# Splitting the fp32 ones-products of a hybrid encoder step into high and low halves

## What is computed

```python
def conv_module_tail(glu, hist, conv_w, conv_b, ln_g, ln_b):
    ...
    return jax.nn.silu(layer_norm(y, ln_g, ln_b))      # mean and variance over 512 channels

def finish_layer(h, att, cv, p, w_out, g_ffn, w_gate_up, w_down, g_ple, w_ple_gate, w_ple_proj):
    h = h + jnp.concatenate([att, cv], axis=-1) @ w_out
    u = rms_norm(h, g_ffn)                             # mean square over 1024 channels
    gate, up = jnp.split(u @ w_gate_up, 2, axis=-1)
    h = h + (jax.nn.silu(gate) * up) @ w_down
    g = jax.nn.sigmoid(rms_norm(h, g_ple) @ w_ple_gate)
    return h + g * (p @ w_ple_proj)
```

## Time and profile before

| | us |
|---|---|
| median of 3 runs | 2595.95 (2593.81 to 2599.28) |
| the profiled execution | 2596.51 |
| its span, first to last instruction | 2594.8 |
| TensorE busy | 2576.0 |
| VectorE busy | 1847.3 |
| ScalarE busy | 1266.1 |

### The profile page before, as it was taken

One profiled execution on the slowest core, in us unless ns is written; L12 is line 12 of the kernel. 1 busy time (PEld: TensorE's weight loads), 2 busy tenths in 40 slices (PEclk: granted clock), 3 DMA queues, 4 the chain that ended last, 5 costly groups with the idle time before them and its releaser, 6 DMA issues.

```text
span 2594.8 us, 39909 instructions
## 1 busy us (share of the span) xinstructions
PE 2576.0 (99%) x13920; PEld 2501.2 (96%) x13920; DVE 1847.3 (71%) x3391; ACT 1266.1 (49%) x2282; POOL 590.1 (23%) x660
## 2 busy tenths in 40 slices
PE   9999999999999999999999999999999999999999
PEld 8999998999899999999999999999999999999999
DVE  3555579988878888777766877789438765766557
ACT  5444368888864323443334443423446443443465
POOL 6222212121111332323333333233300011111000
PEclk9999999999999999999999999999999999999999
DMA  5667798888677998998898798899895566665676
GB/s 204 212 215 244 233 364 272 281 284 271 203 243 251 298 308 278 301 349 289 317 319 308 273 341 304 302 321 320 290 336 187 163 189 184 188 196 178 201 234 187
DMA packets 316882, 677.12 MB, mean 261 GB/s; under 512 B 37484, under 2 KB 174572, under 8 KB 316140
## 3 DMA queue, kind: packets, MB, share of 16 engines
q1 hardware_dynamic: 295324, 603.78, 69.9%
q0 software_dynamic: 21360, 70.80, 7.6%
HBM read 512.19 MB, written 164.29 MB: 261 GB/s over the span
## 4 chain that ended last, share of the span: by engine, by line
PE 83%; DVE 6%; DMA 5%; issue 2%; ACT 2%; SPq 2%; POOL 0%; DVEq 0%; ACTq 0%; POOLq 0%
PE psum L198 51%; PE psum L2546 24%; PE psum L1551 2%; PE psum L1526 2%; DMA x<-in_w_gu 1%; PE psum L1513 1%; DMA a_cr<-in_cache 1%; PE psum L1514 1%; DVE y L3150 1%; DVE wres L3103 1%; DVE ul L685 1%; DMA ul<-ul_d 1%; SPq L1115 0%; DMA ql_d<-a_room 0%; POOL wres L628 0%
## 5 line engine op out<-in xcount | busy, mean ns | idle before, releaser
L198 PE MATMUL psum<-uh,wres 128*128 128x416 f32 x3936 | 1118.8, 356 | 4.3 <-issue 1.8
L198 PEld LDWEIGHTS psum<-uh,wres 128*128 128x128 f32 x3936 | 737.4, 188 | 17.0 <-issue 3.9
L198 PE MATMUL psum<-ul,wres 128*128 128x416 f32 x1968 | 688.2, 350 | 0.0
L2980 ACT ACTIVATE wres<-x 128x1024 fp32r<-128x1024 f32 (+2 forms) x234 | 268.7, 1148 | 633.3 <-PE psum L198 550.5
L198 PE MATMUL psum<-wres 128*128 128x416 f32 x2304 | 447.5, 352 | 1.8 <-DVE wres L1360 0.6
L198 PEld LDWEIGHTS psum<-wres 128*128 128x128 f32 x2304 | 430.7, 188 | 8.8 <-issue 2.8
L2546 PE MATMUL psum<-wres 128*128 128x416 f32 x2104 | 426.1, 352 | 1.0 <-DVE c_top L2465 0.6
L2546 PEld LDWEIGHTS psum<-wres 128*128 128x128 f32 x2104 | 393.6, 188 | 6.5 <-ACT wres L1712 1.7
L198 PEld LDWEIGHTS psum<-ul,wres 128*128 128x128 f32 x1968 | 370.8, 188 | 6.4 <-issue 1.4
L3150 DVE SCALAR_TENSOR_TENSOR y<-c_top,vec,y 128x416 f32<-128x416 f32 (+1 forms) x600 | 342.0, 638 | 0.8
L1712 ACT ACTIVATE wres<-c_top 128x512 fp32r<-128x512 f32 (+1 forms) x302 | 181.4, 602 | 129.2 <-PE psum L2546 49.7
(11 more groups left out here) (306 smaller groups left out, 3617.5 us busy)
## 6 DMA issues: line engine op xcount, KB each, us to landing
x<-in_w_gu SPq DMA_DIRECT2D x132, 512.0 KB, 5.1
wres<-w_gu_lo SPq DMA_DIRECT2D x88, 512.0 KB, 5.8
c_top<-w_gu_sums SPq DMA_DIRECT2D x136, 256.0 KB, 3.2
x<-in_w_down SPq DMA_DIRECT2D x48, 704.0 KB, 6.1
w_gu_sums<-c_top POOLq DMA_DIRECT2D x60, 512.0 KB, 6.0
w_gu_lo<-wres SPq DMA_DIRECT2D x44, 512.0 KB, 6.4
c_top<-in_w_gu POOLq DMA_DIRECT2D x88, 256.0 KB, 5.7
wres<-w_down_lo SPq DMA_DIRECT2D x32, 704.0 KB, 7.1
```

What stands on the lines that cost most here:

```text
L198: mm = nc.tensor.matmul(out, w[wp](kw), u[up](ku), start=first and n == 0 and j == 0, stop=last and n == len(kts) - 1 and j == 2)
L2980: nc.scalar.activation(whi[v % 2][:, 0:kts, :], raw[v % 2][:, 0:kts, :], ACT.Copy).then_inc(hi_done, 1)
```

## The change

In the single blocks each product of ones with an fp32 vector becomes two fp32r products, of the vector's high and of its low part. ScalarE makes the high part (`sum_high`, `total_high`), VectorE the low part (`sum_low`, `total_low`), and the strided reduction becomes three adds, each waiting for the one before. The parts lie in unused places of `c_hx` and `c_between`.

```diff
@@ scalar engine
+            def sum_high(b, i):
+                act.wait_ge(sum_out, sum_count(b, i, KD - 1))
+                nc.scalar.activation(sum_hi, ssum[:, :], ACT.Copy).then_inc(sq_out, 1)
+
+            def total_high(n, i):
+                act.wait_ge(cv_sum, (CT + 1) * total_count(n, i) + CT - 1)
+                nc.scalar.activation(total_hi, csum[:, :], ACT.Copy).then_inc(cv_sum, 1)
...
                     act.wait_ge(p_in, 16 * (b + 1))
                     nc.scalar.activation(ph[:, :, :], p[:, :, :], ACT.Copy).then_inc(p_hi, 1)
+                    sum_high(b, 0)
...
+                    for i in range(2):
+                        if early(u) and u["f"] == STEPS[early(u)]["total"][i]:
+                            total_high(early(u), i)
...
                 elif kind == "D" and u["half"]:
+                    if late(u) and u["m"] in (1, 6):
+                        total_high(late(u), int(u["m"] == 6))
                     tile_out(b, 1, u["m"], V_GPLE, u["left0"] + 1)
...
+                    if u["m"] == KD - 1:
+                        sum_high(b, 1)
@@ vector engine
             def cv_sum_up(n, i, src):
-                nc.vector.tensor_reduce(out=csum[:, :], in_=src[:, :, :].rearrange("p c n -> p n c"),
-                                        axis=AX.X, op=ALU.add).then_inc(cv_sum, 1)
+                for ct in range(1, CT):
+                    if ct > 1:
+                        dve.wait_ge(cv_sum, (CT + 1) * total_count(n, i) + ct - 1)
+                    nc.vector.tensor_tensor(csum[:, :], csum[:, :] if ct > 1 else src[:, 0, :], src[:, ct, :],
+                                            ALU.add).then_inc(cv_sum, 1)
+
+            def total_low(n, i):
+                dve.wait_ge(cv_sum, (CT + 1) * total_count(n, i) + CT)
+                nc.vector.tensor_tensor(total_lo, csum[:, :], total_hi.bitcast(F32), ALU.subtract).then_inc(cv_sum, 1)
+
+            def sum_low(b, i):
+                dve.wait_ge(sq_out, sq_count(b, i, KD) + 1)
+                nc.vector.tensor_tensor(sum_lo, ssum[:, :], sum_hi.bitcast(F32), ALU.subtract).then_inc(sum_out, 1)
...
                 if first_tile(u):
+                    sum_low(b, int(kind == "P"))
                     weight_low(v + 2)
                     norm(b, int(kind == "P"))
...
                         hidden_low(b, u["half"], u["f"] - 1)
+                    for i in range(2):
+                        if early(u) and u["f"] == STEPS[early(u)]["total"][i]:
+                            total_low(early(u), i)
...
                             n = late(u)
+                            if m in (1, 6):
+                                total_low(n, int(m == 6))
@@ tensor engine
             def norm(b, i):
-                pe.wait_ge(sum_out, sum_count(b, i, KD - 1))
+                pe.wait_ge(sum_out, sum_count(b, i, KD))
                 if b or i:
                     pe.wait_ge(n_sd, 2 * b + i)
-                nc.tensor.matmul(ps_n[:, 0:N], c["ones"][:, :], ssum[:, :], start=True, stop=True).then_inc(n_mm, 1)
+                nc.tensor.matmul(ps_n[:, 0:N], ones_r, sum_hi, start=True, stop=False)
+                nc.tensor.matmul(ps_n[:, 0:N], ones_r, sum_lo, start=False, stop=True).then_inc(n_mm, 1)
 
             def cv_total(n, i):
-                pe.wait_ge(cv_sum, (n - 1) * 2 + i + 1)
-                nc.tensor.matmul(ps_c[:, 0:N], c["ones"][:, :], csum[:, :], start=True, stop=True).then_inc(cv_mm, 1)
+                pe.wait_ge(cv_sum, (CT + 1) * (total_count(n, i) + 1))
+                nc.tensor.matmul(ps_c[:, 0:N], ones_r, total_hi, start=True, stop=False)
+                nc.tensor.matmul(ps_c[:, 0:N], ones_r, total_lo, start=False, stop=True).then_inc(cv_mm, 1)
```

More of the change, by code:

```diff
@@ L1932, in last_pair @@
     u_hi, u_lo, sq_out, sum_out = (f[e] for e in ("u_hi", "u_lo", "sq_out", "sum_out"))
-    T0, Q0, A0 = 2 * SINGLE * KD, (2 * SINGLE + 1) * KD, (2 * SINGLE + 1) * (KD - 1)
+    T0, Q0, A0 = 2 * SINGLE * KD, (2 * SINGLE + 1) * KD + 2 * SINGLE, (2 * SINGLE + 1) * KD - 1
     n_mm, n_sd, n_r, NN = f["n_mm"], f["n_sd"], f["n_r"], 2 * SINGLE
@@ L2778, in finish @@
         csum, csd, crs = (tile((20 + e) * N + 4 * KH * P) for e in range(3))
+        sum_hi, sum_lo = c["hx"][:, 3 * KP, :], c["hx"][:, 3 * KP + 2, :]
+        total_hi, total_lo = (c["between"][:, (5 + e) * N + 4 * KH * P:(6 + e) * N + 4 * KH * P] for e in range(2))
+        ones_r = c["ones"][:, :].bitcast(F32R)
         psum = c["psum"]
@@ L2807, in tile_count, with sq_count, total_count @@
             return (2 * b + i) * KD + m
+        def sq_count(b, i, m):
+            return tile_count(b, i, m) + 2 * b + i
         def sum_count(b, i, m):
-            return (2 * b + i) * (KD - 1) + m
+            return (2 * b + i) * KD + m
+        def total_count(n, i):
+            return 2 * (n - 1) + i
         def sig_count(b, kind, n):
@@ L3169, in tile_out @@
                 if m:
-                    dve.wait_ge(sq_out, tile_count(b, i, m) + 1)
+                    dve.wait_ge(sq_out, sq_count(b, i, m) + 1)
                     if m >= 2:
@@ L3188, in first_sum @@
                 if m:
-                    dve.wait_ge(sq_out, tile_count(SINGLE, 0, m) + 1)
+                    dve.wait_ge(sq_out, sq_count(SINGLE, 0, m) + 1)
                     if m >= 2:
```

## The result

The change makes the kernel slower: 2604.49 us (median of 9 runs, 2599.05 to 2606.98) against 2597.11 (9 runs, 2593.81 to 2599.28). The ratio is 1.0029, with a 95% interval of 1.002 to 1.0037, so +7.5 us (+5.2 to +9.6) where +2.9 was forecast, above the forecast's range (2595 to 2602.3). The profiled execution took 2606.84 us with a span of 2605.1, 10.3 more than the span before.

A forecast was written before the change was run, and what follows sets the result against it. TensorE was taken as the bound. Stalls at four norms lose 6.1 us, the other ten places save 3.1, net +3.0; on the median, 2595.95 + 2.9 = 2598.8 us, range 2595 to 2602.3 for 8 in 10.

The forecast's parts named there:

- The bound: Whole kernel: TensorE is busy for 2576.0 of 2594.8 us, so a microsecond counts only if it is TensorE's.
- the price of a product: At 14 places an fp32 product of 0.69 us becomes two fp32r of 0.38, saving 0.31 each, 4.3 us over all.
- the hidden work: ScalarE's copies (8 us), VectorE's subtractions (8 us) and 10 us back from reductions count only where TensorE waits for them.
- The four waits: TensorE loses 1.8, 0.4 and 0.4 us at first norms of blocks 0, 1, 2, and 3.5 at block 1's second.
- The fourth: First norm of block 2: TensorE waits about 0.5 us for VectorE's low part and loses 0.4 us.
- The closest of the other ten: First total of block 1's convolution: a stall between nothing and 1.0 us, taken as nothing.
- a sign of being wrong: Convolution totals in the changed kernel's profile: the forecast is wrong if one of them waits.
- The step that failed: Block 1's second norm: the 3.5 us stall is shorter than the some 4 us idle ending in 1.2 GHz; nothing added.
- rival C: After the idle time at block 1's second norm the clock is halved, 3.3 us more, 2602.1 us; chance 0.07.
- No second stall follows: Behind the norms' waits: the unit's first result is wanted only four units on (two among P units), so nothing added.

The follow-up runs named there:

- second run: The changed kernel with TensorE's six norm products issued one unit later; 1.0023 against the kernel before, +6.0 us.
- seventh run: The changed kernel with first norms back in fp32, second norms' low part made ahead of the taps, totals split; 0.9987 against the kernel before, -3.4 us.
- sixth run: The kernel before, products still fp32, with TensorE's six norm products issued one unit later; 1.0037 against the kernel before, +9.6 us.
- tenth run: The kernel before with block 1's second norm on TensorE waiting for the first two of six taps; 1.0001 against the kernel before, +0.3 us.

## Why the prediction was wrong

**The bound, the price of a product, the hidden work: right.** TensorE bounds the kernel. The rows show two fp32r products in 0.38 us, and the two runs with only the cheap places split agree with 0.31 saved for each (-2.9 for 8 products, -3.4 for 11, each good to some 2.3 us). No cost of the copies and subtractions showed apart from the waits for them, and no gain from VectorE's relief.

**The four waits: right in place, nearly in size.** 2.38, 0.48, 3.54 and 1.53 us were measured for 2.5, 0.5, 3.5 and 0.5. The fourth was mis-sized by 1 us. Its rows came from one execution in which GpSimd had nothing to do at that moment; so it was in the run with the low part ahead of the taps, and there this wait was 0.1 us. That GpSimd is the cause was not tried. The closest of the other ten, forecast between 0 and 1.0 and taken as nothing, was 0.29; by the forecast's own words such a wait at a total was a sign of being wrong, if a cheap one.

**The step that failed is the clock's.** The sum had no term for what the granted clock does behind the stall of 3.5 us. The text took the moment at which the clock fell after the last matmul, some 4 us, as the idle time that it takes, found the new stall shorter, and gave rival C 0.07. One such moment bounds nothing: in the changed kernel the clock fell 2.7 us into one gap (the 0.62 of the stretch from 1481 puts the fall at 1481.2) and 2.1 us into the other (788.3), and block 0's first norm was not even considered. The trace of the kernel before could have told: at about 653 TensorE waited 1.32 us and, after 0.8 of work, 1.79, and the clock was at half from 655.3 to 658.7 (PE's rows, then the stretches):

```profile
652.18 0.84 PE L198 MATMUL psum<-b_more,wres 128*128 128x416 f32 x3 [1.32 <-DMA b_more<-ul_d]
654.81 0.43 PE L198 MATMUL psum<-uh,wres 128*128 128x416 f32 x1 [1.79 <-issue]
```

```profile
654.00:656.00 2.00, 1.19 (x5) 1.21 (x6) 0.00 (x0) 0.00 (x0) 1.56 (x2) 0.83 1.07 364
656.00:658.00 2.00, 2.00 (x9) 1.71 (x8) 1.13 (x3) 0.00 (x0) 0.00 (x0) 0.50 1.07 384
```

Rival C was the true course for both long waits. Its price of 3.3 us for one came near the 2.7 and 1.4 measured, but by luck: the 32 products that it was read from the earlier trace rows ran at a granted clock of 1.00, and their 0.20 us each is what 128 columns cost at the full clock if 416 columns in fp32 cost 0.69. The forecast's 2.9 with the clock's 4.1 gives 7.0, against 7.5 measured (+5.2 to +9.6). The run with the lone wait shows the clock's loss without the rest of the change, and in the runs with busy work it is gone although the waits end as late, so it comes from the idleness and not from the lateness. The Trainium skill ("TensorE: Matmul & The Clock Gate", section "The HAM clock gate") has it that an idle TensorE falls back to half rate. The trace agrees for the two long waits (0.50 behind 2.38 and 3.54 us), and the forecast weighed it too lightly.

**"No second stall follows" was right where it was said, and not as a rule.** Behind the change's waits the other waits grew by 0.7 us only. Moved by a whole unit, the same root held up high parts of weights, and that cost 9.6 us.

**What stays open.** The saving in time from keeping TensorE busy rests for the change on two comparisons whose intervals overlap (3.1 us, from +7.5 to +4.4), and is not shown by itself for the lone wait; what is shown in both cases is that the clock's loss goes. What decides whether the clock falls after a wait of about 2 us is open. Why the waits for weights in block 0 differ from one profile to the next (from 0.4 to 1.9 us at about 1034) was not tried. The lowest time was measured with only the second norms and the totals split: 2593.8 us beside 2596.1 of the kernel before, 3.4 less by the ratio. Splitting only the totals (2.9 less) can't be told from it.

## What to carry to other kernels

A wait of the engine that bounds the kernel has two prices: its length, and for TensorE what it takes afterwards at the lower clock. Here the second was about as large as the first for a wait of 3 us (3.1 and 3.1). When an operand gets one more step on another engine, look up what stands in that engine's queue between the old last step and the new one, and put the new step ahead of it; and before moving the waiting instruction itself, look at what waits for its result at the head of a third engine's queue.

## What was not expected of the hardware

Waits of up to 1.53 us by themselves left the granted clock full where it was looked at, and those of 3.13 and 3.54 us were followed by a stretch at half of it. In between it went both ways: behind 1.82 us (second run, at 1110), 1.92 (seventh run) and 2.38 (block 0 of the change) the clock was halved, behind 2.08 (sixth run, at 886) and 2.39 (tenth run, at 1135) it stayed full. No limit can be read from these. Nor is it a matter of the kernel alone: the drop at about 655 that the kernel before shows stands in 9 of the 13 profiles. The fall does not have to come inside the wait: in the kernel before with the wait for six taps TensorE was back at work at 1481.54, and the clock fell at about 1482.8 (the 0.69 of 1482 to 1484). Nor does the stretch end soon after TensorE is busy again, and its length changes: after the wait of 3.54 us it lasted from 1481.2 to 1488.0, 6.8 us, after that of 2.38 us 3.4. And a VectorE subtraction of 416 columns took 0.58 us with GpSimd idle and 1.11 with GpSimd at work beside it, in the same execution.
